# Two transformer blocks on one core: the residual stream with its features on partitions, side work placed by a clock of TensorE time

## The chip, the cores and the metric

One core of a Trainium2 chip runs the whole program in one launch. The metric is the device time of that launch in microseconds, the median of several runs. All arithmetic is fp32 to the outside.

## The reference

One batch of 512 tokens with 1024 features goes through two blocks. The parts that matter here, shortened:

```python
mem_n = rmsnorm(mem, mem_norm)
# layer A (mLSTM)
h = rmsnorm(x, a_norm)
qk, v, o, z, i_pre, f_pre, mq, mz = split_cols(h @ a_w_in, ...)
ht = mlstm_chunkwise(q, k, v, i_pre + ig_b, f_pre + fg_b)      # 4 heads of 256
x = x + concat(sigmoid(o) * rmsnorm(ht) * silu(z), memory_attention(mq, mz, mk, mv)) @ a_w_out
# layer B (MLA)
c_kv, k_pe = split_cols(rmsnorm(x, kv_norm) @ w_kv_a, ...)     # k, v of 8 heads from the latent
q_lat, z, mq, mz = split_cols(rmsnorm(x, b_norm) @ b_w_in, ...)
x = x + concat(chunk_causal_attention(q, k, v) * silu(z), memory_attention(mq, mz, mk, mv)) @ b_w_out
# second block
u, q, k, v, gates = split(rms_norm(x, g_mix) @ w_in, ...)
x = x + (concat(causal_multiscale_pool(u), rms_norm(diff_attention(q, k, v))) * sigmoid(gates)) @ w_out
x = x + memory_cross_attention(rms_norm(x, g_cross), rms_norm(mem_2, g_mem))
x = x + square(relu(rms_norm(x, g_mlp) @ w_up)) @ w_down       # 4096 wide
return rms_norm(x, g_final)
```

A norm multiplies each token by 1/sqrt(mean of its squares) and each feature by a gain. memory_attention and cross attention see 256 memory tokens.

## The kernel before

**Products.** Every large product is an entry of product_table: a weight, its columns, its source and a form. Weights come in chunks of two k tiles (128 rows of the weight each); SP fetches a chunk into one of two raw buffers, ScalarE writes its upper half (split, hi), VectorE the rest (lo = raw - hi), into one of three w_split slots. The source (hA, hB, ...) lies in actA or actB as hi and lo too, with features on partitions. For every k tile and every one of up to four output blocks, TensorE does three matmuls: hi hi, hi lo, lo hi. In "feature" form the weight block is stationary and the result has features on partitions; in "token" form the source block is stationary and the result has tokens on partitions. The four blocks of a product fill the PSUM banks 0 to 3 and are evicted (ev) when the last k tile is done.

**The residual stream** x_res is 128 x 4 x 1024: tokens on partitions, four token tiles. The residual products (outA, outB, outC, outD, dn0 to dn3, two halves each) are in token form and are added to it; ScalarE sums the squares of each block as it lands (rsq). Before the next layer each feature tile must be turned: turn is four transposes (two for the memory's 256 tokens) on TensorE (line L1019, in turn_over), then ScalarE writes hi from PSUM, times the feature gain (L1330), and VectorE lo (L1720). The factor per token is applied after the product: nsum makes the mean, POOL takes the power -0.5 (L2267), and where tokens lie along the free axis, ndiag and nrow (a diagonal times a matrix of ones) spread it over all partitions into row[norm].

**Side work** is everything else on TensorE: attention scores, turned probabilities, values, mLSTM rounds, gates. It uses the banks 4 to 7. The names: msc, mtp, mval are scores, turn and values of memory attention; asc, atp, aval of MLA; dsc, dtp, dval of differential attention; csc, ctp, cval of cross attention; hsc, hval, hty of the mLSTM; prep0 to prep6 norm, rotate and turn q and k of a pair of MLA heads; hnsq, hnt, hnsc are head norms; ysplit writes hi and lo of a gated output, the source of outA, outB and outC.

**The order** is written once by order_of_work with a Plan, and all five engines walk through the same list. There are two lanes of side work, each a queue of groups with steps they come after, and a list soon. After each k tile of a product, step puts the first group of soon and at most one group of each lane:

```python
    def step(self):
        if self.soon:
            for step in self.soon.popleft():
                self.put(step)
        for lane in (1, 0):
            self.advance(lane)
```

need(steps) calls step until the steps are there; product calls it for the source tiles of each k tile (hA, hB and the like two tiles ahead). All twelve matmuls of a k tile stand together in TensorE's queue. In rounds, the scores of unit n and the turn of unit n - 1 are one group, with two buffers for probabilities.

**The start:** mem, then x (512 KB per token tile), memT and hA turned, products mk0, mv0, mqA, mzA. The forget gates of the mLSTM need a cumulative sum and a cumulative maximum over 512 tokens; each is nine doubling steps of two VectorE operations over 4 x 512 (cumsum, cummax), one doubling per step of lane 1, and gateT turns the result. **The end:** dn31 is evicted, its squares summed, each token tile scaled and stored.

## Time and profile before

| | |
|---|---|
| median of 3 runs | 1754.74 us (1748.2 to 1758.79) |
| the profiled execution | 1747.94 us |
| its span, first to last instruction | 1746.0 us |
| TensorE busy | 1629.9 us, 7336 matmuls |
| VectorE busy | 889.9 us |
| ScalarE busy | 753.1 us |
| POOL busy | 69.9 us |
| mean granted clock of TensorE | 0.974 |
| HBM read | 138.17 MB, 80 GB/s over the span |

Busy time of TensorE counts overlapping matmuls once; a single matmul's recorded duration reaches into the next one, so costs are read from the distance of starts. "idle before" is time in which the engine had nothing to do, put down to what it waited for. The span ends some 2 us before the execution's own time.

### The profile page before, as it was taken

To read this page: it belongs to the slowest core of one execution; us is meant where nothing else is said; L and a number is where in the kernel's file an instruction comes from. 1 tells how busy PE (TensorE), PEld (TensorE's weight loads), DVE (VectorE), ACT (ScalarE), POOL (GpSimd) and SP (SyncE) were. 2 spreads that over 40 slices of the span, in tenths; PEclk is the share of its full clock that TensorE was granted. 3 is DMA by queue.
4 is the path that set the end of the run, shared out by engine and by line. 5 is a ranking of instruction groups with operands and counts; after the bars stand their busy time and mean duration, and the time that the engine had idled before them with its cause. 6 is when DMAs were issued, how large, how long until landed. Compare 5 with 4: busy or idle time off the path is not lost.

```text
span 1746.0 us, 19776 instructions
## 1 busy us (share of the span) xinstructions
PE 1629.9 (93%) x7336; PEld 1269.4 (73%) x7336; DVE 889.9 (51%) x1879; ACT 753.1 (43%) x1714; POOL 69.9 (4%) x64
## 2 busy tenths in 40 slices
PE   6996999999999978899899999889999999999997
PEld 5574777777787866666678877467786878888886
DVE  4367446738445464555544647445444453434343
ACT  6353333324345556666433343335323443434342
POOL 0011001101000000000000000000000000000000
PEclk9998999999999999999999999689999999999999
DMA  6221222222333211111123222013232323333332
GB/s 202 72 82 37 73 61 73 84 62 86 132 103 115 67 38 50 45 46 47 61 74 108 85 73 85 1 50 108 86 108 79 103 85 98 97 100 95 98 98 78
DMA packets 85119, 141.54 MB, mean 81 GB/s; under 512 B 7200, under 2 KB 32160, under 8 KB 85024
## 3 DMA queue, kind: packets, MB, share of 16 engines
q1 hardware_dynamic: 83728, 137.45, 25.5%
q10 hardware_dynamic: 1296, 2.83, 0.5%
q8 instruction: 58, 0.95, 0.2%
q14 instruction: 37, 0.30, 0.1%
HBM read 138.17 MB, written 2.10 MB: 80 GB/s over the span
## 4 chain that ended last, share of the span: by engine, by line
PE 61%; DVE 13%; issue 13%; ACT 10%; DMA 1%; POOL 1%; ACTq 0%; DVEq 0%; SPq 0%; POOLq 0%
PE banks L1059 10%; PE banks L1061 10%; PE banks L1060 10%; PE banks L1054 7%; PE banks L1056 7%; PE banks L1055 7%; DVE sb_arena L1711 3%; ACT sb_junk L1318 3%; PE banks L1019 3%; DVE sb_arena L1720 2%; DVE sb_w_split L1711 2%; ACT sb_w_split L1355 2%; ACT sb_arena L1484 1%; PE banks L1243 1%; DVE sb_arena L1714 1%
## 5 line engine op out<-in xcount | busy, mean ns | idle before, releaser
L1711 DVE TENSOR_TENSOR sb_w_split<-sb_raw,sb_w_split 128x512 fp32r<-128x512 f32 (+4 forms) x520 | 322.6, 662 | 367.2 <-ACT sb_w_split L1355 366.3
L1355 ACT ACTIVATE sb_w_split<-sb_raw 128x512 fp32r<-128x512 f32 (+4 forms) x520 | 286.1, 600 | 352.7 <-PE banks L1061 193.3
L1059 PE MATMUL banks<-sb_w_split,sb_actB 128*128 128x512 f32 (+2 forms) x752 | 302.3, 402 | 7.2 <-DVE sb_w_split L1711 3.0
L1061 PE MATMUL banks<-sb_w_split,sb_actB 128*128 128x512 f32 (+2 forms) x752 | 291.5, 388 | 0.0
L1060 PE MATMUL banks<-sb_w_split,sb_actB 128*128 128x512 f32 (+2 forms) x752 | 291.2, 387 | 0.0
L1054 PE MATMUL banks<-sb_actA,sb_w_split 128*128 128x512 f32 x672 | 271.9, 405 | 1.6 <-DVE sb_arena L1720 1.5
L1056 PE MATMUL banks<-sb_actA,sb_w_split 128*128 128x512 f32 x672 | 262.9, 391 | 0.0
L1055 PE MATMUL banks<-sb_actA,sb_w_split 128*128 128x512 f32 x672 | 262.5, 391 | 0.0
L1059 PE MATMUL banks<-sb_w_split,sb_actA 128*128 128x512 f32 (+1 forms) x416 | 167.8, 403 | 2.2 <-DVE sb_arena L1720 2.2
L1059 PEld LDWEIGHTS banks<-sb_w_split,sb_actB 128*128 128x128 f32 x752 | 144.0, 192 | 32.9 <-DVE sb_w_split L1711 5.6
L1061 PEld LDWEIGHTS banks<-sb_w_split,sb_actB 128*128 128x128 f32 x752 | 143.1, 190 | 28.2
L1060 PEld LDWEIGHTS banks<-sb_w_split,sb_actB 128*128 128x128 f32 x752 | 143.9, 191 | 25.1 <-issue 0.5
L1061 PE MATMUL banks<-sb_w_split,sb_actA 128*128 128x512 f32 (+1 forms) x416 | 161.2, 387 | 0.0
L1060 PE MATMUL banks<-sb_w_split,sb_actA 128*128 128x512 f32 (+1 forms) x416 | 160.8, 386 | 0.0
L1019 PE MATMUL banks<-sb_cons,sb_arena 128*128 128x128 f32 x508 | 94.6, 294 | 65.8 <-DVE sb_arena L1714 35.9
L1054 PEld LDWEIGHTS banks<-sb_actA,sb_w_split 128*128 128x128 f32 x672 | 126.7, 188 | 27.7 <-issue 3.6
L1056 PEld LDWEIGHTS banks<-sb_actA,sb_w_split 128*128 128x128 f32 x672 | 126.5, 188 | 27.5
L1055 PEld LDWEIGHTS banks<-sb_actA,sb_w_split 128*128 128x128 f32 x672 | 126.8, 189 | 25.4 <-issue 1.0
L1019 PEld LDWEIGHTS banks<-sb_cons,sb_arena 128*128 128x128 f32 x508 | 63.9, 148 | 97.9 <-DVE sb_arena L1714 42.4
L2267 POOL TENSOR_TENSOR sb_small<-sb_small,sb_cons 128x4 f32<-128x4 f32 (+4 forms) x33 | 44.0, 1336 | 1556.0 <-DVE sb_small L1717 1556.0
L1484 ACT ACTIVATE sb_arena<-banks,sb_small 128x256 f32<-128x256 f32 (+2 forms) x80 | 45.3, 567 | 126.6 <-DVE sb_small L1714 126.4
L1059 PEld LDWEIGHTS banks<-sb_w_split,sb_actA 128*128 128x128 f32 x416 | 78.6, 189 | 22.2 <-issue 5.3
(163 smaller groups left out, 1864.1 us busy)
## 6 DMA issues: line engine op xcount, KB each, us to landing
sb_raw<-in_a_w_in SPq DMA_DIRECT2D x64, 256.0 KB, 3.0
sb_raw<-in_w_up SPq DMA_DIRECT2D x32, 512.0 KB, 3.6
sb_raw<-in_w_down SPq DMA_DIRECT2D x32, 512.0 KB, 3.7
sb_raw<-in_w_in SPq DMA_DIRECT2D x24, 512.0 KB, 3.6
sb_raw<-in_mem_w_kv SPq DMA_DIRECT2D x16, 512.0 KB, 3.8
sb_raw<-in_a_w_in SPq DMA_DIRECT2D x16, 512.0 KB, 3.7
sb_raw<-in_w_ckv SPq DMA_DIRECT2D x16, 512.0 KB, 3.7
sb_raw<-in_a_w_out SPq DMA_DIRECT2D x12, 512.0 KB, 3.7
```

The source lines that it names most:

```text
L1019: t = pe.op.transpose(v.ps[0:rows, place.bank, n * P:(n + 1) * P], block, v.ident)
L1054: pe.op.matmul(out, hi[:, cs], x.hi(k), start=i == 0, stop=False)
L1055: pe.op.matmul(out, hi[:, cs], x.lo(k), start=False, stop=False)
L1056: t = pe.op.matmul(out, lo[:, cs], x.hi(k), start=False, stop=last_i)
L1059: pe.op.matmul(out, x.hi(k)[:, cs], hi, start=i == 0, stop=False)
L1060: pe.op.matmul(out, x.hi(k)[:, cs], lo, start=False, stop=False)
L1061: t = pe.op.matmul(out, x.lo(k)[:, cs], hi, start=False, stop=last_i)
L1318: t = act.op.activation(v.junk[:, 0:src.shape[-1]], src, ACT.Square, accum_out=out)
L1355: act.op.activation(hi[:, cs], raw[:, cs], ACT.Copy).then_inc(act.mark(m("w_hi"), 2 * n + part + 1), 1)
L1484: act.op.activation(prob, src, ACT.Exp, bias=v.stat(("mx", step), 1), scale=scale, accum_out=v.stat(("sm", step), 1)).then_inc(act.mark(em ...
L1711: dve.op.tensor_tensor(out, a, b, op).then_inc(dve.mark(*mark) if mark else dve.tick(), 1)
L2267: pool.op.tensor_tensor(v.stat(root, n), v.stat(mean, n), v.con("minus_half", 0, n), ALU.pow).then_inc(m.at("rstd", step)[0], 1)
```

## The change

The residual stream and the three memory inputs are kept with features on partitions (x_res is 128 x 8 x 512; x, mem and mem_2 come transposed from the host, and the output is handed back so). The residual products take the feature form. turn becomes one ScalarE operation (hi, from SBUF) and one VectorE operation (lo). The squares of a feature tile are taken by ScalarE (sqa), added up over the tiles by POOL (sqp) and summed over partitions by matmuls of one column (nsq). The final norm takes the same way, with nrow, and eight stores of a feature tile.

In the order, Plan has a clock: row_ns and side_ns estimate TensorE's time of each row block and each side step, and a group of a lane is put only when its lag has passed since the last one of that lane. The row blocks of a k tile are steps of their own (rows), and a group of one lane can be put between them. need takes only what is missing (force). Units of layer B's attention have two groups between scores and turn, with three buffers; mzB is two products, the products of layer B stand in another order, the sum and the maximum of the gates are one scan each (gateA), mqA is the first product, and x is loaded one feature tile at a time beside the first chunks. ckD1 is before cqD0, and cvD0 and cvD1 are behind cqD1.

The diff, cut to its core (the lists of addresses, buffers and waits that follow from it are left out):

```diff
-    add("mzB", B, D_MODEL, [(B_MZ, 512)], "feature", "hB", "silu")
+    for n in range(2):
+        add(f"mzB{n}", B, D_MODEL, [(B_MZ + n * 256, 256)], "feature", "hB", "silu")
...
-            add(f"{name}{half}", w, nk * P, [(half * 512, 512)], "token", src, "res", order=order, k0=k0)
+            add(f"{name}{half}", w, nk * P, [(half * 512, 512)], "feature", src, "res", order=order, k0=k0)
...
+def row_ns(name):
+
+    pr = PRODUCTS[name]
+    return 3 * n_out(name) * ((pr.tokens if pr.form == "feature" else wide(name)) / 2.4 + 13)
...
+def side_ns(step):
+
+    kind, i = step[0], step[-1]
+    wide_f32, turn = 1.68, 109
+    if kind in ("msc", "mtp"):
+        return 430 if kind == "msc" else 2 * turn
+    if kind in ("csc", "ctp"):
+        return 860 if kind == "csc" else 2 * turn
+    if kind in ("mval", "cval"):
+        return 2 * 860 if kind == "mval" else 4 * 860
+    if kind == "asc":
+        return (i + 1) * P * (wide_f32 + 2.1) + 66
+    if kind == "dsc":
+        return 2 * ((i + 1) * P * 3.0 + 66)
+    if kind in ("atp", "dtp"):
+        return (i + 1) * turn
+    if kind == "dval":
+        return (i + 1) * 224
+    if kind == "hsc":
+        return (TT - i) * P * wide_f32 * 3 + 66
+    if kind == "hval":
+        return (i + 1) * (430 + 224)
+    return {"aval": 10 * P * wide_f32, "gate0": 3440, "gate1": 3440, "gate2": 3440, "gate3": 3440, "pp": 860,
+            "nsq": 900, "nrow": 860, "gateT": 660}.get(kind, TT * turn if kind in EMPTIES else 0)
...
+def squares(norm, n):
+
+    return [("sqa", norm, n)] + ([("sqp", norm, n)] if n and not (norm == "f" and n >= 4) else [])
...
+        self.clock, self.last = 0.0, [0, 0]
...
+        self.clock += side_ns(step)
...
-    def side(self, lane, after, *steps):
-        self.lanes[lane].append((tuple(after), steps))
+    def side(self, lane, after, *steps, lag=2600):
+
+
+        self.lanes[lane].append((tuple(after), steps, lag + (LATER.get(steps[0], 0) if steps else 0)))
+
+    def take(self, lane):
+        self.last[lane] = self.clock
+        for step in self.lanes[lane].popleft()[1]:
+            self.put_side(lane, step)
 
     def advance(self, lane):
-        if self.lanes[lane] and all(a in self.done for a in self.lanes[lane][0][0]):
-            for step in self.lanes[lane].popleft()[1]:
-                self.put_side(lane, step)
+        if self.lanes[lane]:
+            after, steps, lag = self.lanes[lane][0]
+            if all(a in self.done for a in after) and self.clock - self.last[lane] >= lag:
+                self.take(lane)
...
+    def force(self, step):
+
+        if any(step in group for group in self.soon):
+            for s in self.soon.popleft():
+                self.put(s)
+            return
+        lane = next((n for n in (0, 1) if any(step in group[1] for group in self.lanes[n])), None)
+        assert lane is not None, ("nothing to wait for", step)
+        missing = [a for a in self.lanes[lane][0][0] if a not in self.done]
+        if missing:
+            self.force(missing[0])
+        else:
+            self.take(lane)
...
     def need(self, *steps):
-        tries = 0
-        while not all(s in self.done for s in steps):
-            tries += 1
-            assert tries < 1000, ("nothing to wait for", [s for s in steps if s not in self.done])
-            self.step()
-
-    def product(self, name, before_ev=(), soon=None):
+        for step in steps:
+            while step not in self.done:
+                self.force(step)
...
-                banks = [(j, EV_EMPTIES[pr.ev]) for j in range(n_out(name))] if i == 0 else ()
+                banks = [(into[j], EV_EMPTIES[pr.ev]) for j in range(n_out(name))] if i == 0 else ()
                 self.put(("mm", name, i), banks)
+                for j in range(n_out(name)):
+                    self.put(("rows", name, i, j))
+                    self.clock += row_ns(name) / n_out(name)
+                    if j < n_out(name) - 1:
+                        self.advance((i * n_out(name) + j) % 2)
...
+    def after_residual(self, name):
+
+        norm, turn, first = NORM_AFTER[name[:-1]], TURN_AFTER.get(name[:-1]), 4 * int(name[-1])
+        for j in range(first, first + 4):
+            steps = [("turn", turn, j)] if turn else []
+            if first:
+                for step in steps:
+                    self.put(step)
+                self.soon.append(squares(norm, j))
+            else:
+                self.soon.append(steps + squares(norm, j))
...
-    def scales(lane, norm, row=True, after=()):
-        p.side(lane, after, ("nsum", norm))
+    def turns(name, tiles):
+
+        for k in tiles:
+            p.soon.append([("turn", name, k)])
+
+    def scales(lane, norm, row=True, after=(), lag=4000):
+        p.side(lane, after, lag=0)
+        p.side(lane, (), ("nsq", norm), ("nsum", norm), lag=lag)
         if row:
-            p.side(lane, ())
-            p.side(lane, (), ("ndiag", norm))
-            p.side(lane, (), ("nrow", norm))
+            p.side(lane, (), ("ndiag", norm), ("nrow", norm), lag=4500)
...
+        complete, first = None, True
+        for n in range(len(units) + depth):
...
-                group.append((turn_over, *before))
-                if before[-1] == TT - 1:
-                    complete = before[:-1]
-            before = u
-            p.side(lane, after if first else values_after if group[0][0] == values else (), *group)
+            if n < len(units):
+                group.append((scores, *units[n]))
+            if n >= depth:
+                u = units[n - depth]
+                group.append((turn_over, *u))
+                if u[-1] == TT - 1:
+                    complete = u[:-1]
+            p.side(lane, after if first else values_after if group[0][0] == values else (), *group, lag=lag)
             first = False
...
+    for n in range(2):
+        p.put(("load_x", n))
+        p.put(("fetch", n))
+    p.n_fetch = 2
+    p.put(("load_x", 2))
+    p.put(("turn", "hA", 0))
+    p.put(("split", 0))
+    p.put(("fetch", 2))
+    p.put(("load_x", 3))
+    p.put(("turn", "hA", 1))
...
+        p.soon.append(([("turn", "hA", k)] if k >= 2 else []) + squares("a", k))
+    for n in range(4):
+        p.soon.append([("turn", "memT", 2 * n), ("turn", "memT", 2 * n + 1)] + squares("mem", n))
+    p.soon.append([("masks",)])
+    scales(0, "a", after=[("sqp", "a", 7)], lag=0)
...
+    p.product("mqA", [("nsum", "a")])
+    p.ahead = SPLIT_SLOTS
+    scales(0, "mem", row=False, after=[("sqp", "mem", 3)])
+    p.product("mk0", [("nsum", "mem")], into=(5, 7))
...
-    p.side(1, (), ("gateL",))
-    for n in range(9):
-        p.side(1, (), ("cumsum", n))
     p.side(1, (), ("gateA",))
-    for n in range(9):
-        p.side(1, (), ("cummax", n))
-    p.side(1, (), ("gateM",))
-    p.side(1, (), ("gateT",))
-    p.product("mqA", [("nsum", "a")])
-    head_norm(0, "mqA", TT, True)
+    p.side(1, (), ("gateT",), lag=4000)
...
-            p.side(1, after if si == 0 else (), *group)
+            p.side(1, after if si == 0 else (), *group, lag=5000)
...
-    turns(1, "memTb", range(KD))
     p.product("outA0")
-    turns(0, "hB", range(4))
+    p.put(("load_mem_again",))
     p.product("outA1")
 
 
     p.put(("enter", "outA1"))
-    turns(0, "hK", range(KD))
-    scales(0, "b")
+    turns("hK", range(KD))
+    scales(0, "b", after=[("sqp", "b", 7)])
+    for k in range(KD):
+        p.soon.append([("turn", "memTb", k)])
+    p.product("qlB", [("nsum", "b")])
+    for step in (("qll0",), ("qll1",)):
+        p.side(1, (), step, lag=1500)
+    p.product("ckvB")
+    for step in (("kvl0",), ("kvl1",)):
+        p.side(1, (), step, lag=1500)
     p.product("mk1")
-    head_norm(1, "mk1", MT, False)
+    head_norm(0, "mk1", MT, False)
     p.product("mv1")
     for n in range(3):
...
+    def mla(h0):
+
+        units = [(h, j) for h in (h0, h0 + 1) for j in range(TT)]
+        complete = None
+        for n in range(len(units) + 3):
+            group, after = [], []
             if complete is not None:
                 group += [("aval", complete), ("ysplit", "yB", complete)]
+                after.append(("silu", f"zB{complete // 2}", complete % 2))
...
+            if n < len(units):
+                group.append(("asc", *units[n]))
+                after.append(("prep6", h0 // 2))
+            if 2 <= n < len(units) + 2:
+                group.append(("atp", *units[n - 2]))
+                if units[n - 2][1] == TT - 1:
+                    complete = units[n - 2][0]
+            p.side(0, after, *group, lag=2800)
+
+    def mem_b(h0):
+        rounds(0, [("B", h, i) for h in (h0, h0 + 1) for i in range(TT)], "msc", "mtp", "mval",
+               [("hnscale", "mqB"), ("hnt", "mk1", 3)], [("silu", f"mzB{h0 // 2}", 1)], depth=2, lag=2400)
...
-            p.side(1, (), (f"prep{s}", q))
-        p.product(f"zB{q}", (), lambda j: [(("silu", f"zB{q}", j),)])
+        for n in range(7):
+            p.side(1, (), (f"prep{n}", q), lag=2600)
+
+    def gated(name):
+        p.product(name, (), lambda j: [(("silu", name, j),)])
+
+    gated("zB0")
+    p.need(("kpe",))
+    latents(0)
+    p.product("mqB")
+    mla(0)
+    head_norm(1, "mqB", TT, True)
+    mem_b(0)
+    mem_b(2)
+    latents(1)
+    p.need(("nrow", "b"))
+    gated("mzB0")
+    gated("mzB1")
+    mla(2)
+    latents(2)
+    p.need(("mval", "B", 3))
+    gated("zB1")
+    mla(4)
+    latents(3)
+    p.need(("ysplit", "yB", 1))
+    gated("zB2")
+    p.need(("ysplit", "yB", 3))
+    gated("zB3")
+    mla(6)
     for h in range(MEM_HEADS):
...
+        elif kind == "nsq":
+            norm = a[0]
+            tiles, place_full = v.tiles_of[norm], open_bank(step)
+            place, full = place_full
+            blocks = [(v.sq_sum[norm], 0)] if tiles == TT else [(v.sq_sum[norm], 0), (v.sq_sum[norm], N_MEM)]
+            last = SQUARES.get(norm, KD) - 1
+            if norm == "f":
+                blocks += [(v.square_of(norm, n)[1], 0) for n in range(4, KD)]
+                pe.wait_ge(*m.at("sq", ("sqa", norm, last)))
+                last = 3
+            pe.wait_ge(*m.at("sq_sum", ("sqp", norm, last)))
+            for i in range(tiles):
+                for n, (block, at) in enumerate(blocks):
+                    t = pe.op.matmul(v.ps[:, place.bank, i:i + 1], block[:, at + i * P:at + (i + 1) * P], v.con("ones"),
+                                     start=n == 0, stop=n == len(blocks) - 1)
...
+            act.op.activation(dst.hi(k), src, ACT.Copy, scale=gain).then_inc(act.mark(*m.at("t_hi", step)), 1)
+        elif kind == "sqa":
+            norm, n = a
+            src, out = v.square_of(norm, n)
...
+            back = 5 if norm == "f" else 2
+            if n > back:
+                act.wait_ge(*m.at("sq_sum", ("sqp", norm, n - back)))
+            act.op.activation(out, src, ACT.Square).then_inc(act.mark(*m.at("sq", step)), 1)
...
+            dve.wait_ge(*m.at("t_hi", step))
+            fused(dst.lo(k), src, gain, ALU.mult, dst.hi(k).bitcast(F32), ALU.subtract, *m.at("t_lo", step))
...
-        elif kind == "gateA":
-            g = v.gate_rows
+            dve.op.memset(g[7], 1.0).then_inc(dve.tick(), 1)
+            dve.settle()
+            dve.op.tensor_tensor_scan(g[6], g[7], g[5], 0.0, ALU.mult, ALU.add).then_inc(dve.tick(), 1)
             dve.settle()
             tensor(g[1], g[0], g[6], ALU.subtract)
             dve.settle()
-            copy(g[2], g[1])
-        elif kind == "cummax":
-            doubling(a[0], (2, 3), ALU.max)
-        elif kind == "gateM":
-            g = v.gate_rows
-            dve.settle()
-            both(v.neg_m, g[3], 0.0, ALU.max, -1.0, ALU.mult)
+            dve.op.tensor_tensor_scan(g[3], g[1], g[1], 0.0, ALU.max, ALU.max).then_inc(dve.tick(), 1)
+            dve.settle()
+            scalar(v.neg_m, g[3], -1.0, ALU.mult)
...
+        elif kind == "sqp":
+            norm, n = a
+            signal, value = m.at("sq_sum", step)
+            pool.wait_ge(*m.at("sq", ("sqa", norm, n)))
+            if n >= 2:
+                pool.wait_ge(signal, value - 1)
+            total = v.sq_sum[norm]
+            pool.op.tensor_tensor(total, total, v.square_of(norm, n)[1], ALU.add).then_inc(signal, 1)
```

## Rows read from the trace of the kernel before

**Rows 1.** Stretches in us: length; busy PE, PEld, DVE, ACT, POOL; granted clock; DMA share; GB/s.

```profile
0.00:50.00 50.00, 34.14 (x155) 26.91 (x155) 25.79 (x54) 33.77 (x84) 4.32 (x13) 0.97 0.60 194
50.00:200.00 150.00, 131.50 (x530) 94.18 (x529) 83.34 (x192) 61.16 (x144) 9.60 (x5) 0.93 0.21 60
200.00:500.00 300.00, 295.95 (x1336) 231.68 (x1335) 163.91 (x317) 104.96 (x197) 23.08 (x16) 1.00 0.27 84
500.00:850.00 350.00, 312.98 (x1501) 238.47 (x1499) 193.04 (x482) 212.84 (x566) 22.27 (x14) 0.99 0.21 62
850.00:1050.00 200.00, 197.75 (x891) 154.83 (x892) 98.77 (x210) 73.94 (x159) 1.16 (x2) 0.99 0.26 80
1050.00:1150.00 100.00, 89.22 (x328) 59.28 (x327) 58.11 (x147) 33.78 (x95) 3.02 (x3) 0.80 0.13 42
1150.00:1450.00 300.00, 282.30 (x1345) 227.46 (x1344) 142.61 (x285) 119.72 (x255) 4.18 (x7) 0.99 0.29 92
1450.00:1735.00 285.00, 285.00 (x1259) 235.99 (x1258) 118.93 (x182) 107.76 (x205) 0.00 (x0) 1.00 0.29 91
...
sum 1746.00, PE 1629.93 PEld 1269.38 DVE 889.94 ACT 753.07 POOL 69.89; mean PE 181.10 PEld 141.04 DVE 98.88 ACT 83.67 POOL 7.77
```

**Rows 2.** TensorE's timeline at 25 us: start, us, line, form.

```profile
25.00 0.39 PE L1060 MATMUL banks<-sb_w_split,sb_actB 128*128 128x512 f32 x1
25.23 0.39 PE L1061 MATMUL banks<-sb_w_split,sb_actB 128*128 128x512 f32 x1
25.46 0.60 PE L1019 MATMUL banks<-sb_cons,sb_x_res 128*128 128x128 f32 x4
25.81 0.48 PE L1059 MATMUL banks<-sb_w_split,sb_actB 128*128 128x512 f32 x1
26.13 0.40 PE L1060 MATMUL banks<-sb_w_split,sb_actB 128*128 128x512 f32 x1
```

**Rows 3.** TensorE's waits between 500 and 850 us: total, times, longest.

```profile
PE banks L1019 <- DVE sb_arena L1714: 13.0, 7, 3.3
PE banks L1019 <- DVE sb_arena L1711: 10.9, 8, 1.8
```

**Rows 4.** TensorE's timeline at the gates, after 159 us.

```profile
159.79 0.98 PE L1123 MATMUL banks<-sb_cons,sb_arena 4*128 4x4 f32 x8 [3.39 <-DVE sb_arena L1711]
...
162.58 0.63 PE L1060 MATMUL banks<-sb_w_split,sb_actA 128*128 128x512 f32 x1
163.01 0.63 PE L1061 MATMUL banks<-sb_w_split,sb_actA 128*128 128x512 f32 x1
```

**Rows 5.** Groups by line on TensorE: count, busy us, mean ns, idle before.

```profile
L1019 PE MATMUL banks<-sb_cons,sb_x_res 128*128 128x128 f32 x192 | 29.2, 275 | 0.9 <-DVE sb_actA L1720 0.9
...
L1173 PE MATMUL banks<-sb_cons,sb_arena 128*128 128x1 f32 x80 | 9.8, 234 | 0.0
```

**Rows 6.** Timelines of VectorE and POOL while both work on SBUF.

```profile
265.14 2.33 DVE L1720 SCALAR_TENSOR_TENSOR sb_arena<-sb_arena,sb_cols 128x512 f32<-128x512 f32 x3
...
267.96 4.15 DVE L1720 SCALAR_TENSOR_TENSOR sb_arena<-sb_arena,sb_cols 128x512 f32<-128x512 f32 x3
...
268.11 3.45 POOL L2285 TENSOR_TENSOR sb_arena<-sb_arena 128x512 f32<-128x512 f32 x2 [16.56 <-ACT sb_arena L1500]
```

**Rows 7.** Groups by line and shape, on POOL and on VectorE.

```profile
L2267 POOL TENSOR_TENSOR sb_small<-sb_small,sb_cons 128x4 f32<-128x4 f32 x15 | 15.1, 1007 | 846.6 <-DVE sb_small L1717 846.6
...
L1711 DVE TENSOR_TENSOR sb_arena<-sb_arena 4x512 f32<-4x512 f32 x3 | 2.0, 680 | 2.9 <-ACT sb_arena L1460 2.9
```

**Rows 8.** TensorE's timeline in the first stretch: first product, and wait behind mk0.

```profile
14.52 0.80 PE L1059 MATMUL banks<-sb_w_split,sb_actB 128*128 128x512 f32 x1 [3.02 <-DVE sb_w_split L1711]
...
31.65 0.68 PE L1059 MATMUL banks<-sb_w_split,sb_actB 128*128 128x512 f32 x1 [1.93 <-ACT sb_arena L1394]
```

**Rows 9.** Timelines of TensorE and VectorE at the end.

```profile
1735.71 0.39 PE L1061 MATMUL banks<-sb_w_split,sb_actB 128*128 128x512 f32 x1
...
1738.28 2.73 DVE L1720 SCALAR_TENSOR_TENSOR sb_arena<-sb_x_res,sb_small,sb_arena 128x512 f32<-128x512 f32 x4
```

554 lines of the change are left out of this document (254 added, 300 removed).

## The prediction

> **What bounds the kernel now.** I read the profile from the whole to the place. First the table of stages [rows 1]. TensorE is busy 1629.9 of 1746.0 us, and VectorE and ScalarE each about half of that, so only TensorE's queue sets the end: either something leaves that queue, or one of its waits goes. The differences (length less busy) are its idle time: 15.9 us in the first 50 us, 18.5 in 50 to 200, 4.1 in 200 to 500, 37.0 in 500 to 850, 2.2 in 850 to 1050, 10.8 in 1050 to 1150, 17.7 in 1150 to 1450, none in the long MLP stretch; of the 116.1 us in total, 9.9 are left for what follows the last product. The granted clock falls below 1.00 where there are waits: 0.93 in 50 to 200 and 0.80 in 1050 to 1150.
>
> Second, what a product costs when nothing disturbs it: two neighbouring 128x512 matmuls start 0.23 us apart [rows 2]. The same rows price a turn: with four transposes between them, the matmuls of 25.23 and 26.13 are 0.90 us apart where two pitches would be 0.46. The four cost 0.44 us, 0.11 us each, though each is recorded with some 0.27 us (they overlap).
>
> Third, what the waits in the stages are. Between 500 and 850 us nearly all are transposes (line L1019) that wait for VectorE's scaling of a softmax block (L1714, L1711) [rows 3]: 13.0 + 10.9 us. That is a round whose scores, exponentials and turn follow each other in TensorE's queue faster than VectorE and ScalarE get through them. Between 50 and 200 us it is the same kind plus the forget gates: TensorE stands 3.39 us before the turn of the gate rows, and what follows then runs at the low one of the clock's two levels, 1.2 instead of 2.4 GHz: pitch 0.43 us [rows 4].
>
> **The change part by part, against the profiled span of 1746.0 us.**
>
> *Transposes of the normalised streams go.* With features on partitions, turn is one ScalarE and one VectorE operation from SBUF; TensorE has no part in it. Removed are 8 x 2 for each of memT, memTb and m2T and 8 x 4 for each of hA, hB, hK, hC, hD, hE: 48 + 192 [rows 5] = 240. Eight of them lie in the idle start. 232 x 0.11 = -25.5 us, in the open, since TensorE is otherwise busy there. The residual products keep their count and size; only the operands change sides, the same stationary block still serves two matmuls of three: 0. On the other engines a turn keeps its two operations, and the sums of squares of dn0 to dn2, which nobody reads, go: less work on ScalarE, behind TensorE, 0.
>
> The Trainium skill (TensorE: Matmul & The Clock Gate, Part 4: PE-mode transpose) gives about 275 ns for a 128x128 transpose in one kernel. The records agree with that length, the pitch does not: by 0.275 the 232 would be worth an estimated 64 us instead of 25.5.
>
> *Sums of squares over partitions come.* Seven norms ahead of the last get nsq: 28 matmuls of one column. The one-column matmuls of this trace are recorded with 0.234 us [rows 5]; the pitch of a short one is nearer 0.11. 3.1 to 6.6 us; I take +3, since they have a transpose's weight load. ScalarE squares into a ring, POOL adds: 7 adds for each of a to e, 3 for f, mem and m2, 44 in all. A 128x512 POOL operation took 1.7 us beside VectorE, and three VectorE operations beside two of these took 4.15 us where three took 2.33 alone [rows 6]: 0.9 us of VectorE per add, 40 us spread over the kernel. VectorE is idle half of the time [rows 1], and the weight split runs two to three chunks (5.4 us each) ahead of TensorE: I take 0 for it; with the cover gone, at a border where evictions, turns and splits queue behind each other, up to 4 x 0.9 at five borders, +18.
>
> The Trainium skill (SBUF — State Buffer, SBUF: two separate sides) says that a VectorE operation with two SBUF inputs and a GpSimd operation that reads SBUF exclude each other for the whole instruction. The new VectorE half of turn, the split and ysplit are all of that form. By that rule each add could hold VectorE for its full 1.7 us, an estimate of 75 us of VectorE time instead of 40; still hidden while VectorE has half its time free.
>
> *The chain behind each residual.* Four evictions, squares, adds, nsq, nsum, the POOL root (1.0 us, [rows 7]), ndiag, nrow must be through before the next product is evicted. Cover: kC and up00 have 96 matmuls, 21.8 us; qlB 96 of 384 columns, about 16.6; ckD0 of 256 tokens about 11, and with it m2's squares, put last. Two places force their nsq and nrow into the end of the product: I count +3 at ckD0 and 0 elsewhere; it is in the term of 1150 to 1450. In return the first tiles no longer wait for turns there.
>
> *Start.* TensorE's first product begins at 14.52 [rows 8], after 1 MB of mem, eight turns of one bank lane and the split. Afterwards it waits for one 256 KB tile of x, one chunk and its split. The core moved 194 GB/s on average in this stretch [rows 1]; x, cons and the first chunk, some 1.2 MB, land about 6 us in, the split adds 2.5: about 8.5. -6 us, and -1 for the 1.9 us wait behind mk0. Bounds 0 (loads stay the limit: mqA needs 0.5 MB per 2.7 us of products, 190 GB/s, as much as was moved) and -11.
>
> *50 to 200 us.* Cumsum and cummax, 36 dependent VectorE operations over 4x512, one pair per tile of TensorE's order, become two scans. The trace has no scan; its price is bounded by one operation (0.68 us, [rows 7]) and by the 18 x 0.68 that it replaces. One is nearest in shape; the gates are then ready long before ozA0. The memory rounds take 4.4 us of TensorE time per group instead of 2.7 plus their own. Of 18.5 idle I take 15, and 5 more for the low clock: -20 (bounds -8, -25).
>
> *500 to 850 us.* The mem rounds of layer B get two groups between scores and turn, three buffers for probabilities, and lie behind the first MLA heads; MLA likewise; prep is spread. A chain waits for ScalarE and VectorE for 1 to 3.3 us a time, and one more group of 2.4 to 2.8 us covers that. Of 37.0 I take 29, and 2 for the clock: -31 (bounds -10, -36). If the cover fails, it is in outB0, where the last heads are forced: then they wait there.
>
> *1050 to 1150 us.* The differential attention still waits for gateG of gC0 and is then forced before outC0: the burst stays. -3 (0 to -10). *1150 to 1450:* turns at two borders, cross attention over both lanes. Of 17.7 I take 12, less 3 at ckD0: -9 (+3 to -15). *200 to 500, 850 to 1050, MLP:* 6.3 us idle, 0.
>
> *Tail.* The last matmul starts at 1735.71 [rows 9] and ends 0.23 later: 10.1 us to the end. Afterwards: eviction 0.7, square 0.6, 20 one-column matmuls 2.2, nsum 0.3, root 1.0, ndiag 0.9, nrow 1.1, its copy 0.6, eight stores at 0.69 (four took 2.73, [rows 9]) 5.5, last landing 3, hand-overs 1: 17. +7 (5 to 10), all open.
>
> **Sum:** -25.5 + 3 - 7 - 20 - 31 - 3 - 9 + 7 = -85.5, so a span of 1660.5. The profiled execution took 1747.94, 1.9 more than its span: 1662.4, a ratio of 0.951. The median before is 1754.74; by the ratio 1669, by the difference to the lower one 1662. I say 1665.
>
> **Rivals.**
> *A, the order helps half:* the chains stay bound by VectorE's and ScalarE's own queues, in front of which evictions and splits stand, and only the low ends (8, 10) of the two large terms come. 1665 + 12 + 21 = 1698. For: VectorE is at 50 to 60% in both windows, and POOL's adds come on top. Against: waits are at most 3.3 us, less than a group.
> *B, the places are worth nothing:* what is forced by need stands as before. Only turns, start, sums and tail: -25.5 + 3 - 7 + 7 = -22.5, 1729.
> *C, more:* nearly all inner idle time and low clock go, 15 to 40 us beyond the forecast: 1637.
> *D, transposes cost TensorE their recorded length* [rows 5] where the trace's pitch is not looked at: 232 x (0.27 - 0.11) = 37 more, 1628. Against it is the pitch of [rows 2]. (It is the case that the 275 ns of the Trainium skill, TensorE: Matmul & The Clock Gate, would give.)
> *E, slower:* the norm chain is not covered at the five residual borders. It decides when a chain overruns its product by more than 85.5/5 = 17 us at each; with 20 us, 1665 + 100 = 1765. That needs a chain of 36 us and more; its parts above sum to about 10, and with both lags of 4.0 and 4.5 us to 20.
>
> **Chances.** Forecast (1645 to 1688) 0.58; A 0.18; B 0.06; C 0.10; D 0.02; E 0.04; about no change 0.02. The bounds of the terms alone give 1630 to 1718; range 1628 to 1705, which leaves out B, E, the no-change case and the far ends. 0.5% (9 us) is what a measurement of this kernel tells from no change: faster 0.94, same 0.02, slower 0.04.
>
> **What would show it.** No L1019 rows from x_res or mem (right); the next products' pitch still 0.23; idle time of 500 to 850 under 10 us; no wait before gateT; start of the first product before 10 us; tail of 15 to 20 us. Wrong would be: long waits of TensorE for nsq or nrow, splits late behind POOL's adds (a wait on w_split's lower half), or new waits in outB0 and outC0.

## Result, and the profile after

The changed kernel took **1784.7 us** (median of 4 runs, 1784.0 to 1787.7); the kernel before, timed beside it, took 1754.2. The ratio is **1.0178, 95% interval 1.0149 to 1.0206**: 30 us slower. Forecast was 1665 us, faster. The profiled execution took 1784.0 us with a span of 1782.2.

The same stretches of the changed kernel as in [rows 1], with the same columns:

```profile
50.00:200.00 150.00, 127.96 (x509) 91.86 (x508) 74.12 (x152) 67.59 (x158) 10.42 (x6) 0.93 0.25 69
200.00:500.00 300.00, 298.68 (x1331) 232.94 (x1329) 168.35 (x328) 104.10 (x199) 26.00 (x19) 1.00 0.28 83
500.00:850.00 350.00, 308.08 (x1395) 232.06 (x1393) 194.86 (x487) 209.24 (x567) 28.88 (x18) 0.94 0.21 59
...
1150.00:1450.00 300.00, 277.41 (x1260) 220.99 (x1260) 151.16 (x290) 113.82 (x241) 30.62 (x25) 0.95 0.28 85
...
sum 1782.00, PE 1648.46 PEld 1274.07 DVE 911.12 ACT 732.44 POOL 132.27; mean PE 206.06 PEld 159.26 DVE 113.89 ACT 91.55 POOL 16.53
```

Read it against [rows 1]. The idle time of 500 to 850 us is 41.9 us, not under 10 (before: 37.0); in 50 to 200 it is 22.0 (18.5); in 1150 to 1450 it is 22.6 (17.7). The granted clock fell in two of the three, 0.99 to 0.94 and 0.99 to 0.95; in 50 to 200 it stayed at 0.93. And TensorE is busy 18 us *longer* with 142 matmuls fewer.

Fixed stretches mix up stages as soon as one kernel runs ahead, so for all that follows I cut both traces by products: TensorE's timeline gives the start of each product's first matmul, the program's order says which product it is, and a stage is the distance between two such starts. Each distance from one matmul's start to the next is booked on product, side work or, where the timeline shows a wait, idle time. In us (the last column is the best version found, e15 below):

| stage | before | changed | difference | e15 |
| --- | --- | --- | --- | --- |
| start to qkA1 | 223.3 | 216.3 | -7.0 | 210.0 |
| qkA1 to layer B | 288.0 | 283.7 | -4.3 | 285.2 |
| layer B to outB0 | 324.9 | 344.4 | **+19.5** | 329.4 |
| outB0, outB1 | 92.8 | 90.6 | -2.2 | 90.0 |
| layer C | 274.1 | 277.8 | +3.7 | 273.0 |
| layer D | 180.1 | 191.4 | **+11.3** | 182.3 |
| MLP to dn31 | 331.0 | 335.5 | +4.5 | 328.7 |
| dn31 to the end | 31.8 | 42.5 | **+10.7** | 39.8 |
| sum | 1746.0 | 1782.2 | +36.2 | 1738.4 |

By kind, from the same cut, in us:

| | before | changed | e15 |
| --- | --- | --- | --- |
| up to the first product | 14.5 | 8.0 | 8.0 |
| product matmuls | 1307.9 | 1337.0 | 1316.9 |
| side work | 320.0 | 304.0 | 302.7 |
| idle | 93.3 | 112.8 | 92.6 |
| from the last product matmul's start | 10.3 | 20.4 | 18.3 |

Idle time is here what the profile puts before TensorE's matmuls between the first and the last product. In the side work, all transposes on TensorE together fell from 73.7 us (700 of them) to 49.7 (460): 24.0 for the 240 that left (eight of them before the first product), near the 25.5 that I forecast. Of the 29 us by which product matmuls rose, 17 are at the low clock (distance between starts over 0.36 us; the time above 0.227 each sums to 19.7 before, 37.2 after). Layer B's 19.5 us are 7.7 of idle time, 1.3 of side work and 10.5 in product matmuls, nearly all of it at the low clock (0.4 before, 10.7 after).

The three places where the loss shows best are these. TensorE's timeline in quB2, where the rest of layer B's memory rounds is forced (7 of the 16 units stand there, and quB2 takes 26.9 us in place of 13.5):

```profile
714.49 0.41 PE L1214 MATMUL banks<-sb_w_split,sb_actB 128*128 128x384 f32 x1 [2.74 <-ACT sb_arena L1588]
...
726.56 0.66 PE L1172 MATMUL banks<-sb_cons,sb_arena 128*128 128x128 f32 x2 [1.97 <-ACT sb_arena L1646]
728.75 3.75 PE L1304 MATMUL banks<-sb_actB_plain 128*128 128x512 f32 x4 [1.53 <-ACT sb_actB_plain L1656]
...
737.37 0.69 PE L1172 MATMUL banks<-sb_cons,sb_arena 128*128 128x128 f32 x2 [1.47 <-DVE sb_arena L1869]
```

TensorE's in ckD0, the norm of the second memory, and under it POOL's timeline of that moment:

```profile
1233.62 1.83 PE L1241 MATMUL banks<-sb_cons,sb_arena 128*128 128x1 f32 x8 [9.30 <-POOL sb_arena L2404]
1237.27 1.19 PE L1250 MATMUL banks<-sb_arena 128*128 128x256 f32 x2 [1.81 <-DVE sb_arena L1869]
1239.48 0.55 PE L1209 MATMUL banks<-sb_actB,sb_w_split 128*128 128x256 f32 x1 [1.02 <-DVE sb_arena L1866]
```

```profile
1224.76 8.71 POOL L2404 TENSOR_TENSOR sb_arena<-sb_arena 128x512 f32<-128x512 f32 x6 [3.63 <-ACT sb_arena L1550]
```

Six adds in a row, 1.45 us each: three for the residual's own norm (d), then the three of the second memory, for the last of which TensorE waits. They start late, too. ScalarE's timeline just before shows the squares of the residual behind a weight split whose weights had not landed:

```profile
1223.01 1.16 ACT L1509 ACTIVATE sb_w_split<-sb_raw 128x512 fp32r<-128x512 f32 x2 [4.31 <-DMA sb_raw<-in_w_ckv]
1224.07 1.13 ACT L1550 ACTIVATE sb_arena<-sb_x_res 128x512 f32<-128x512 f32 x2
```

And the tail; with [rows 9]:

```profile
1761.84 0.40 PE L1211 MATMUL banks<-sb_actB,sb_w_split 128*128 128x512 f32 x1
1763.73 5.25 PE L1241 MATMUL banks<-sb_cons,sb_arena 128*128 128x1 f32 x40 [1.49 <-issue]
1771.48 2.04 PE L1250 MATMUL banks<-sb_arena 128*128 128x512 f32 x2 [2.51 <-POOL sb_arena L2406]
```

I had counted 20 one-column matmuls, 2.2 us. They took 5.25 us, 0.26 us each; each shows as two records.

### The profile page after: what moved, and what is told of

It reads as the page before. It is cut to its first block, busy times and chain, and to the rows that moved or that the text cites. A ratio compares the mean times of both kernels' runs of the same rounds, so it can differ in the third digit from the quotient of the medians.

```text
span 1782.2 us, 19350 instructions
## 1 busy us (share of the span) xinstructions
PE 1648.5 (92%) x7194; PEld 1274.1 (71%) x7194; DVE 911.1 (51%) x1853; ACT 732.4 (41%) x1619; POOL 132.3 (7%) x106
## 4 chain that ended last, share of the span: by engine, by line
PE 71%; DVE 13%; ACT 8%; issue 4%; DMA 2%; POOL 1%; ACTq 0%; DVEq 0%; POOLq 0%; SPq 0%
PE banks L1209 15%; PE banks L1211 15%; PE banks L1210 15%; PE banks L1214 5%; PE banks L1216 5%; PE banks L1215 5%; DVE sb_arena L1866 3%; DVE sb_w_split L1866 3%; PE banks L1172 2%; ACT sb_junk L1477 2%; DVE sb_arena L1875 2%; PE banks L1401 2%; ACT sb_arena L1646 1%; ACT sb_w_split L1509 1%; DMA sb_raw<-in_mem_w_kv 1%
## 5 line engine op out<-in xcount | busy, mean ns | idle before, releaser
L1866 DVE TENSOR_TENSOR sb_w_split<-sb_raw,sb_w_split 128x512 fp32r<-128x512 f32 (+3 forms) x530 | 339.3, 682 | 392.6 <-ACT sb_w_split L1509 391.2
L1509 ACT ACTIVATE sb_w_split<-sb_raw 128x512 fp32r<-128x512 f32 (+3 forms) x530 | 288.0, 593 | 469.0 <-PE banks L1211 359.7
L1209 PE MATMUL banks<-sb_actA,sb_w_split 128*128 128x512 f32 x672 | 276.8, 412 | 6.4 <-DVE sb_arena L1866 3.1
L1211 PE MATMUL banks<-sb_actA,sb_w_split 128*128 128x512 f32 x672 | 264.7, 394 | 0.0
L1210 PE MATMUL banks<-sb_actA,sb_w_split 128*128 128x512 f32 x672 | 263.9, 393 | 0.0
L1209 PE MATMUL banks<-sb_actB,sb_w_split 128*128 128x512 f32 (+1 forms) x640 | 255.4, 399 | 5.6 <-DVE sb_actB L1866 2.2
L1211 PE MATMUL banks<-sb_actB,sb_w_split 128*128 128x512 f32 (+1 forms) x640 | 249.6, 390 | 0.0
L1210 PE MATMUL banks<-sb_actB,sb_w_split 128*128 128x512 f32 (+1 forms) x640 | 249.3, 389 | 0.0
L1214 PE MATMUL banks<-sb_w_split,sb_actA 128*128 128x512 f32 (+1 forms) x384 | 157.0, 409 | 12.6 <-DVE sb_w_split L1866 9.1
L1209 PEld LDWEIGHTS banks<-sb_actA,sb_w_split 128*128 128x128 f32 x672 | 127.9, 190 | 36.2 <-issue 10.0
L1215 PE MATMUL banks<-sb_w_split,sb_actA 128*128 128x512 f32 (+1 forms) x384 | 151.5, 394 | 0.0
L1216 PE MATMUL banks<-sb_w_split,sb_actA 128*128 128x512 f32 (+1 forms) x384 | 151.2, 394 | 0.0
L1209 PEld LDWEIGHTS banks<-sb_actB,sb_w_split 128*128 128x128 f32 x640 | 123.7, 193 | 34.2 <-issue 6.5
L1211 PEld LDWEIGHTS banks<-sb_actA,sb_w_split 128*128 128x128 f32 x672 | 127.3, 189 | 27.7
L1210 PEld LDWEIGHTS banks<-sb_actA,sb_w_split 128*128 128x128 f32 x672 | 127.9, 190 | 25.5 <-issue 1.5
L1210 PEld LDWEIGHTS banks<-sb_actB,sb_w_split 128*128 128x128 f32 x640 | 123.4, 193 | 26.8 <-issue 1.4
L1211 PEld LDWEIGHTS banks<-sb_actB,sb_w_split 128*128 128x128 f32 x640 | 123.0, 192 | 27.0
L1172 PE MATMUL banks<-sb_cons,sb_arena 128*128 128x128 f32 x460 | 83.7, 292 | 47.2 <-DVE sb_arena L1869 16.9
L2404 POOL TENSOR_TENSOR sb_arena<-sb_arena 128x512 f32<-128x512 f32 x44 | 64.9, 1477 | 710.2 <-ACT sb_arena L1550 707.2
L1172 PEld LDWEIGHTS banks<-sb_cons,sb_arena 128*128 128x128 f32 x460 | 58.7, 149 | 70.6 <-issue 22.6
L2395 POOL TENSOR_TENSOR sb_small<-sb_small,sb_cons 128x4 f32<-128x4 f32 (+3 forms) x30 | 41.8, 1394 | 789.8 <-DVE sb_small L1872 740.9
```

The costliest lines, as they stand in the source:

```text
L1172: t = pe.op.transpose(v.ps[0:rows, place.bank, n * P:(n + 1) * P], block, v.ident)
L1209: pe.op.matmul(out, hi[:, cs], x.hi(k), start=i == 0, stop=False)
L1210: pe.op.matmul(out, hi[:, cs], x.lo(k), start=False, stop=False)
L1211: t = pe.op.matmul(out, lo[:, cs], x.hi(k), start=False, stop=last_i)
L1214: pe.op.matmul(out, x.hi(k)[:, cs], hi, start=i == 0, stop=False)
L1215: pe.op.matmul(out, x.hi(k)[:, cs], lo, start=False, stop=False)
```

## The experiments

Ratios are to the kernel before, timed beside each run; the changed kernel's is 1.0178. e1 to e8 ran on one chip, e9 to e11 on a second, e12 to e14 on a third and e15 on a fourth, so across these groups the ratios compare better than the medians.

| run | median us | ratio | 95% interval |
| --- | --- | --- | --- |
| e1 pace of before | 1779.2 | 1.0148 | 1.0124 to 1.0173 |
| e2 no places | 1768.7 | 1.0088 | 1.0062 to 1.0114 |
| e3 second memory's sums first | 1777.4 | 1.0143 | 1.0122 to 1.0165 |
| e4 layer B's old order | 1801.3 | 1.0276 | 1.0255 to 1.0298 |
| e5 actA and actB exchanged | 1759.6 | 1.0044 | 1.0027 to 1.0061 |
| e6 rounds of B spread | 1763.1 | 1.0064 | 1.0042 to 1.0086 |
| e7 gates earlier | 1760.7 | 1.0044 | 1.0021 to 1.0068 |
| e8 POOL's sums twice | 1774.6 | 1.0127 | 1.0103 to 1.0150 |
| e9 actB where it was, tail | 1746.1 | 0.9961 | 0.9944 to 0.9979 |
| e10 gates and B mended | 1753.4 | 1.0008 | 0.9993 to 1.0022 |
| e11 e9 and e10 | 1743.0 | 0.9945 | 0.9927 to 0.9962 |
| e12 wide cover for B | 1739.4 | 0.9923 | 0.9903 to 0.9942 |
| e13 before, 136 transposes less | 1742.9 | 0.9942 | 0.9920 to 0.9965 |
| e14 before, 240 transposes more | 1770.8 | 1.0096 | 1.0073 to 1.0120 |
| e15 best order | 1737.2 | 0.9916 | 0.9898 to 0.9934 |

**e1 and e2: the pace, and the places.**

```diff
-                    if j < n_out(name) - 1:                       # e1 and e2
-                        self.advance((i * n_out(name) + j) % 2)
-            if all(...) and self.clock - self.last[lane] >= lag:  # e1 only
+            if all(...):
```

> The changed kernel with the pace of the kernel before: a group of each lane is released after every k tile, whatever the clock says, and none between the row blocks of a k tile. Product order, layout and norm steps stay as changed. Theory 1 (the lags and the places between row blocks are what went wrong: they hold side work back until a product needs it all at once): the 19.5 us that layer B lost and most of the extra low-clock time (17 us) come back, 1745 to 1760 us, against 1784.7 for the changed kernel. Theory 2 (the pace is worth what it was meant to be, and layer B lost its time to the new order of its products): bursts of short work make it slower still, 1795 to 1815 us. Theory 3 (neither: layout and norm chains cost it): within 8 us of 1784.7.

> Lags kept, but no group is placed between the row blocks of a k tile: groups come only at the end of a k tile, when their lag has passed. Theory 1 in the form that the places break up the products (each place leaves two short pieces of product and a gap in which the clock falls): 1765 to 1775 us, with fewer stretches of product matmuls at 0.43 us. Theory 2 (places help): 1790 to 1800 us. Theory 3: within 5 us of 1784.7.

e1 took 1779.2, e2 1768.7 us. None of the theories has it right for both: e1 lies where theory 3 had it, e2 where theory 1 had it, but the time at the low clock, which theory 1 wanted down, hardly fell (37.2 to 34.8 us). The places between row blocks cost: without them the ratio is 0.0090 lower, 16 us. By stages, 10 of them came before qkA1 (qkA0 took 47.6 us in place of 54.0, vA0 30.8 in place of 37.1), 4 each in layers B and C, and qkA1 to layer B gave 3 back. In layer C the places are what made TensorE wait: kC, qC and vC took 24.2, 23.8 and 24.3 us in e2, as before, and in the changed kernel 27.7, 25.9 and 27.6, with these waits:

```profile
955.46 2.05 PE L1250 MATMUL banks<-sb_arena 128*128 128x512 f32 x2 [2.31 <-DVE sb_arena L1869]
976.48 0.66 PE L1172 MATMUL banks<-sb_cons,sb_arena 128*128 128x128 f32 x4 [2.07 <-DVE sb_arena L1866]
1002.46 0.73 PE L1172 MATMUL banks<-sb_cons,sb_arena 128*128 128x128 f32 x4 [2.10 <-DVE sb_arena L1866]
```

As I read it, a place in the middle of a k tile brings a group forward, in front of the last row blocks that would have covered its chain; no run shows this apart. The lags, on the other hand, help: e1 differs from e2 by them alone and is 10.5 us slower. Layer B did not come back in either (344.2 and 340.7 us).

**e3: the order of two sums on POOL.**

```diff
-    for n in range(4):
-        p.soon.append(squares("m2", n))
+    p.soon.extendleft([squares("m2", n) for n in (3, 2, 1, 0)])
```

> The squares of the second memory are put ahead of the squares of the residual at the start of layer D. The 9.30 us wait of the first one-column matmuls of that norm behind POOL's sums in ckD0 goes away if the order of POOL's queue was its cause: ckD0 from 26.6 to 16 to 18 us, the kernel 1774 to 1778 us. If the wait was for the arrival of the memory's data instead, ckD0 stays at 25 to 27 us and the time at 1783 to 1786. Should the wait move on to the residual's own norm (first used by cqD0, two products later), cqD0 gets an idle time over 3 us.

The wait of 9.30 us is gone, ckD0 took 18.9 us, layer D 181.4 in place of 191.4, and the ratio fell by 0.0035, 6 us. The order in which the squares and sums are queued was the cause. It is not all POOL's: ScalarE's wait of 4.31 us for the weights, which had held up the residual's squares and with them the sums of m2, is now 0.92 and behind m2's squares. In the new order a turn of m2T came late instead (TensorE waited 2.01 us for it), and waits of 2.58 us for the row (nrow) and 1.02 behind it stayed.

**e4: layer B's old order** (mqB and mzB ahead of the latents, one round behind, all in lane 0).

> Layer B's order of products and of side work is taken back as far as the buffers allow (all memory rounds in lane 0, turned over one unit after their scores, products mqB and mzB ahead of the latents, attention turned over one unit late), with the new lags and places. Theory 2 (the new order of layer B costs it 19.5 us): layer B from the start of qlB to outB0 falls from 344.4 to about 325 us, the kernel to 1763 to 1768 us. Theory 1 (the pace costs it): layer B stays at 340 to 350 us, the kernel within 6 us of 1784.7.

Layer B took 354 us, 10 more: the rounds then have to end in quB0, which took 49.1 us (15.0 idle). Theory 2 as I had put it fell. The new order was not the loss as a whole. In the changed layout the old one cannot be had: the allocation puts the turned probabilities into actB, where ckvB's operand hK still is, so that the rounds can begin only when ckvB is through; before, ckvB stood beside 6 of the 16 units. qlB, which stood beside 8, is free of that (e12 below puts it there).

**e5 to e8** stand on e2 and e3 together, a base that was not run alone.

> From here on the base is the changed kernel with e2 and e3 together: no places between row blocks, the second memory's squares first. If the two add up, that base runs about 1768.7 - 7 = 1762 us. On it, this run exchanges the addresses of the two buffers of split activations in SBUF, and nothing else. In the changed kernel a down product takes 22.4 us (pitch 0.2333 us) and an up product 21.8 us (0.2267), both in feature form; before, both took 21.8. Theory A (the address of the moving operand sets the pitch): after the exchange up products take 22.4 and down products 21.8 us. Theory B (it is what else runs during down products, the residual's adds and squares): nothing changes, down 22.4, up 21.8. Theory C (the distance between the two operands or which of them lies lower): both change or both become alike.

TensorE's timeline of the changed kernel in an up product, then in a down product:

```profile
1599.90 0.39 PE L1210 MATMUL banks<-sb_actA,sb_w_split 128*128 128x512 f32 x1
...
1600.58 0.39 PE L1210 MATMUL banks<-sb_actA,sb_w_split 128*128 128x512 f32 x1
...
1639.65 0.39 PE L1210 MATMUL banks<-sb_actB,sb_w_split 128*128 128x512 f32 x1
...
1640.35 0.40 PE L1210 MATMUL banks<-sb_actB,sb_w_split 128*128 128x512 f32 x1
```

and of e5:

```profile
1589.82 0.40 PE L1206 MATMUL banks<-sb_actA,sb_w_split 128*128 128x512 f32 x1
...
1590.52 0.39 PE L1206 MATMUL banks<-sb_actA,sb_w_split 128*128 128x512 f32 x1
...
1634.93 0.39 PE L1208 MATMUL banks<-sb_actB,sb_w_split 128*128 128x512 f32 x1
...
1635.61 0.39 PE L1208 MATMUL banks<-sb_actB,sb_w_split 128*128 128x512 f32 x1
```

Three pitches are 0.68 us from actA and 0.70 from actB in the changed kernel, and the other way round in e5. Over whole products: up 21.8 and down 22.4 became up 22.4 and down 21.8. Theory A holds, to the last product: the pitch goes with the place in SBUF. Products in token form, which hold actA still and move the weights, rose too (ozA1 24.45 us in e2 and in the changed kernel, 25.06 in e5).

> On the same base, layer B's products in the order qlB, ckvB, mqB, mk1, mzB0, mv1, mzB1, then the latents of each pair of heads and its zB, so that the memory rounds of layer B start at the end of mzB0 and are over at the end of quB0, none of them forced; the norms of mqB and mk1 are spaced 1.2 us, the memory rounds 1.2 us. The theory that layer B lost its 19.5 us to the burst that is forced in quB2 (26.9 us for a product of 6.5, 9.7 of them idle) and to rounds that follow each other too closely there: the stretch from qlB to outB0 falls from 340.8 us (e2) to 320 to 328 us and the kernel to 1742 to 1750 us. The rival, that the side work of layer B waits for ScalarE and VectorE wherever it stands: the stretch stays at 335 to 345 us, the idle time moves to mv1, mzB1 and quB0.

The theory fell in this form: layer B took 346.8 us. Nothing was forced, but mv1 took 32.6 us with 11.1 idle and kvB0 waited 6.83 us. Part of that was my own order: the rotary tables stood among the rounds, and the latents right before their reader.

> On the same base, the loads of the gate weights go ahead of mk0 and the gates' matmuls, scans and transposes go behind mk0, ahead of that product's norm, so that they run during mv0 and mzA in place of qkA0. The theory that layer A gained nothing in the stretch 50 to 200 us because mk0 and mv0 now run with no side work beside them and everything waits in qkA0 and ozA0: the waits at gateT (3.3 us) and before msc and hval there (6 us) go, outA0 starts at 402 to 408 us instead of 413, the kernel 1752 to 1757 us. The rival, that the memory rounds wait for the softmax on ScalarE and VectorE whatever the gates do: outA0 at 411 to 415 us and the time at 1760 to 1764.

The time was that of e5, 1760.7 against 1759.6 us. The stretch from the first product to ozA1 took 244.2 us, against 240.6 in e5, and outA0 began at 418.6 us, later than either case had it. The waits at the gates went, and as much came in mzA, where a bank waited 5.58 us to be read out by VectorE, which was busy with the gates' scans. VectorE's work is only moved.

> On the same base, GpSimd makes each of its 44 additions of squares a second time (384 of 512 columns, into a buffer that nobody reads), some 50 us of additional work on GpSimd beside VectorE. My prediction costed GpSimd's sums at nothing. If that holds, the kernel stays within 4 us of its base (1762 us). If GpSimd's additions delay VectorE's work that TensorE waits for, or the norm chains wait for the last sum, each of the six chains gets 1 to 2 us longer and the kernel 1768 to 1780 us; half of such a rise would then be in the changed kernel too.

The upper case: 15 us slower than e5, 14 than e7. e5 also has the two buffers exchanged, so the stages are better read against e2, and ckD0 against e7: the first product mqA +3.4, qlB +5.8, kC +3.6, ckD0 +3.6, up00 +0.3, outD0 0. These are the borders. At qlB (2.87 us) and kC (1.74) TensorE waits for the last sum:

```profile
510.48 1.84 PE L1238 MATMUL banks<-sb_cons,sb_arena 128*128 128x1 f32 x8 [2.87 <-POOL sb_arena L2407]
```

At mqA and ckD0 it waits for VectorE's own work, a weight split (2.93 us, 1.17 in e2) and a turn's lower half (3.54, 2.07 in e7), both stretched beside POOL's adds: the two split halves before the first of these waits took 2.98 us, 2.06 in e2.

**e9: actB back behind actA, and the last norm's sums in four banks.** The first half of the edit moves the allocation of actB from the end to its place before; the second is

```diff
+    for n, (block, at) in enumerate(blocks):       # one wait per block, not one for all
+        if n: pe.wait_ge(*m.at("sq", ("sqa", norm, n + 3)))
+        for i in range(tiles): pe.op.matmul(v.ps[:, 4 + i, 0:1], ...)
```

> On the base of e5 to e8 two edits that act in different stretches. First, the second buffer of split activations (actB) goes back to where the kernel before had it in SBUF, right behind actA, and the weights' buffers go up by its size; in the changed kernel it lay at the end. e5 showed that the slow pitch (0.2333 us against 0.2267) goes with the place. Theory A (a buffer at the far end is read more slowly, one near the start is not): up, down and out products all at 0.2267, a down product 21.8 us, outA1 and outB1 32.6, together 9 to 11 us less. Theory C (one of the two buffers is always the slow one): down stays at 22.4 or up becomes so, 0 us. Second, the last norm: the sums over the 128 partitions of the five blocks are kept in four banks of their own, so that all but the last block's are made before the last square is there. The run of 40 one-column matmuls in 5.25 us behind the last square becomes 8 in about 1.1 us: the tail from the start of dn31 goes from 42.5 to about 38.5 us. Both together: 1759.6 - 10 - 4 = 1745 to 1748 us; 1755 to 1757 if theory C holds.

1746.1 us, 13.5 less than e5 (14.5 by the ratios). Up, down and out products all run at 0.2267 us (21.8 us; outA1 and outB1 32.6). The tail came to 40.2 us, not 38.5: its 20 matmuls (40 records) now begin right behind the last product and still end 5.13 us later.

```profile
1725.92 5.13 PE L1242 MATMUL banks<-sb_cons,sb_arena 128*128 128x1 f32 x40
1733.60 2.05 PE L1258 MATMUL banks<-sb_arena 128*128 128x512 f32 x2 [2.56 <-DVE sb_arena L1877]
```

They are not bound by the last square, as I had thought: it ended at 1727.47, 3.6 us before the last of them. The loads of their 40 blocks fill the same time, 5.26 us. The tail gave 2.3 us, which leaves 11 for the place of the buffer, against e5, where actA stood at the end. e10 and e11 differ by the same two edits, with actB at the end in e10, on one chip: 10.4 us, of which the tail has 3.3. So the place of actB is worth 7 to 11 us.

> On the base of e5 to e8, the orders of e6 and e7 with their own faults mended. In e7 gateT came one k tile behind gateA and waited 5.6 us; it now comes behind the norm of mk0. In e6 the rotary tables (8 loads of ScalarE's table) stood among the memory rounds, which waited 5.2 and 2.7 us for ScalarE, and the turned latents came right before the product that reads them (6.8 us); now the tables go beside mqB and the latents beside mzB1. Theory (orders can take back what layers A and B lost): outA0 at 400 to 405 us against 413 to 418; layer B from qlB to outB0 at 322 to 330 us against 340; the kernel 1735 to 1742 us. Rival (with the buffers of the changed layout, layer B has only narrow products beside its memory rounds, and stands at 340 whatever the order): layer B 337 to 345 us, waits between mv1 and quB0 of 10 us or more, the kernel 1750 to 1756 us.

Between the two: 1753.4 us. Layer B took 334.6 us, the first product to ozA1 242.1 (240.6 in e5, nothing gained). The expectation had misread one row of e7: the wait of 5.6 us was that of mzA's bank, not gateT's, and with gateT later it was there again.

> e9 and e10 together, with e2 and e3 in it: the version that the runs so far point to. If the parts add up it stands at 1720 to 1730 us if e10's theory holds, and at 1736 to 1742 us if its rival does; either beats the kernel before (1751 to 1754 us) and the changed kernel (1784.7 us). If moving the weights' buffers up slows the token products (their moving operand is the weights), they show 0.2333 us in place of 0.2267 and the gain of e9's first half is halved.

1743.0 us; the parts (13.5 and 6.2 us less than e5) add up but for 3 us. The products in token form, which move the weights, kept their pitch (ozA1 24.45 us). Here is what paces a memory round, from ScalarE's and VectorE's timelines in mv1:

```profile
595.96 0.42 DVE L2085 TENSOR_REDUCE sb_small<-banks 128x1 f32<-128x256 f32 x1 [0.22 <-PE banks L1295]
596.42 0.21 DVE L1874 TENSOR_SCALAR sb_small<-sb_small 128x1 f32<-128x1 f32 x1
596.73 0.57 ACT L1651 ACTIVATE sb_arena<-banks,sb_small 128x256 f32<-128x256 f32 x1 [1.30 <-DVE sb_small L1874]
597.42 0.16 DVE L2089 RECIPROCAL sb_small<-sb_small 128x1 f32<-128x1 f32 x1 [0.79 <-ACT sb_arena L1651]
597.62 0.35 DVE L1874 TENSOR_SCALAR sb_arena<-sb_arena,sb_small 128x256 f32<-128x256 f32 x1
...
598.68 0.42 DVE L2085 TENSOR_REDUCE sb_small<-banks 128x1 f32<-128x256 f32 x1
```

Each unit is a chain over both engines, 2.7 us from one reduction to the next, with a weight split between. TensorE's own share of a unit is about 1 us, so by this estimate a unit wants some 1.7 us of product beside it, or TensorE waits.

> The version of e11 with one more product moved in layer B: mqB first, and qlB (three sources wide, 17.5 us) between mv1 and mzB1, beside the memory rounds, which are spaced 2.0 us in place of 1.2. In e11 a unit of the memory rounds takes 2.2 to 2.7 us of ScalarE and VectorE in turn, and the rounds stand beside 35 us of narrow products; in the kernel before they stood beside ckvB, qlB and kvB0, 38 us wide. Theory (what is left of layer B's loss is cover: too little product time beside the rounds): the idle time from mzB0 to quB0 (19.9 us in e11) falls to 8 to 12 us, layer B to 322 to 327 us, the kernel to 1732 to 1738 us. Rival (the units are spaced by ScalarE and VectorE, and what is gained at the rounds comes back where their work is late, at the latents and the softmax behind them): layer B 330 to 336 us, the kernel 1740 to 1746 us.

1739.4 us, layer B 329.1 (333.7 in e11): between the two cases in both. The idle time from mzB0 to quB0 fell only from 15.9 to 14.0 us by the profile, not to 8 to 12, and there is a new wait of 7.51 us at mzB0 for ScalarE, in which the rotary tables stood.

> e12 with two corrections that its trace asks for. The rotary tables, whose table loads kept ScalarE from reading out mk1 (7.51 us of waiting at the start of mzB0), go beside ckvB, spread by 4.2 us; and the gates go back to where the changed kernel has them, since e7, e10, e11 and e12 all took 240 to 245 us up to qkA1's end against 239 to 241 with the gates late. If the two waits go and nothing comes in their place: layer B at 322 to 325 us against 329.3, the first 240 us 1 to 3 us shorter, the kernel 1731 to 1735 us. If ScalarE is the bound there and only the place of the wait changes: ckvB grows from 14.1 us to 18 or more and the kernel stays at 1737 to 1741 us.

1737.2 us, the best of all, 2.6% faster than the changed kernel (0.9916/1.0178 = 0.974) and 0.8% faster than the kernel before. But layer B stayed, at 329.4: the wait at mzB0 went from 7.51 to 4.32 us, and what it gave came back in ckvB (0.7 us), mv1 (1.3) and the products behind zB0. Neither case of the expectation holds: ckvB took 14.8 us, not 18, and with the gates back in their place the first product to ozA1 took 242.4 us, 1.2 more than in e12 and not 1 to 3 less. TensorE's longest waits between 500 and 850 us in the best version, and in the changed kernel under them (total, times, longest):

```profile
PE banks L1166 <- DVE sb_arena L1871: 9.1, 3, 3.9
PE banks L1166 <- ACT sb_arena L1651: 5.6, 2, 3.0
PE banks L1166 <- ACT sb_arena L1747: 4.7, 4, 1.9
```

```profile
PE banks L1172 <- ACT sb_arena L1646: 10.3, 9, 2.4
PE banks L1214 <- ACT sb_arena L1588: 5.0, 3, 2.7
PE banks L1172 <- DVE sb_arena L1866: 4.7, 3, 2.9
```

**e13 and e14: the price of a transpose, in the kernel before.**

```diff
-            turn_over(step, [src[:, i, k * P:(k + 1) * P] for i in range(tiles)])
+            pe.op.transpose(v.ps[:, place.bank, i * P:(i + 1) * P], src[...], v.ident)   # e13: only the last i
```

> The kernel before, in which each step that turns a tile of the residual or of the second and third memory on TensorE makes only the last of its transposes (1 of 4, or 1 of 2; the memory's and x's first ones stay whole). 136 of the 232 transposes are left out, so three quarters of each turned tile hold old data; all other work, waits and the order stay. My prediction took each transpose at 0.11 us of the path. If that holds, the time falls by 136 x 0.11 = 15.0 us, to about 1738 us. If the transposes stood in gaps that ScalarE and VectorE set anyway, or kept the clock up, the time falls by less than 5 us.

> The kernel before, in which each such step makes all its transposes twice (232 more, same output). By the price of 0.11 us each on the path: 25.5 us slower, about 1778 us. If the transposes mostly fill gaps: 5 to 12 us slower. Together with e13 this gives the price of one transpose from both sides; the gain that I forecast from their removal rests on it.

136 fewer: 9.3 us less, 0.068 us each (by the interval 6 to 14 us). e14's edit doubles every turn, the eight before the first product with them, so it adds 240 and not 232 (7576 matmuls in its profile, 7336 before): 18.7 us more, 0.078 each (13 to 21). Both lie between my two cases. In the stream the four cost 0.44 us [rows 2]. Where the rest of that price went shows in e13's profile against that of the kernel before, one execution each, cut as above: 14.9 us of side work left, and 6.5 came back in the product matmuls (3.1 at the low clock) and 1.8 as idle time.

## Why the prediction was wrong, step by step

Of its signs, three came: no turns on TensorE from x_res or mem, the first product before 10 us, and, at the edge of 15 to 20 us, a tail of 20.1 behind the last product's end. Three did not: the idle time of 500 to 850 us, the wait before gateT, and the pitch (0.23 from actB as well, but 3% longer, which two decimals hide). Of its signs of being wrong two came, the long wait for nsq (9.30 us) and, once and small, a split late behind POOL's adds (1.14 us at 17.21); outB0 and outC0 wait no longer than before (2.9 and 9.6 us, 3.6 and 10.4).

- **Transposes go, -25.5.** The mechanism is right and the side work fell by 24.0 us. As a gain it was too large: 232 at 0.068 to 0.078 us are 16 to 18 us (e13, e14). The other 7 to 10 us did not come; in e13's profile most of what was missing stood in the product matmuls.
- **Sums over partitions, +3.** Mis-sized: the seven norms' 28 one-column matmuls took 7.4 us (5.7 in e15), 0.20 us each at the full clock.
- **Start, -6.** Right: the first product starts at 8.00 us (forecast 8.5; before 14.52 [rows 8]).
- **50 to 200 us, -20.** Failed: start to layer B gained 11.3 us in all, start and transposes with it. The step said "the gates are then ready long before ozA0". A scan took 1.21 us (bounds 0.68 to 12.2), and the seven VectorE operations that end with the gates' rows 5.6 together, but TensorE still waited 4.59 us:

```profile
127.12 0.98 PE L1281 MATMUL banks<-sb_cons,sb_arena 4*128 4x4 f32 x8 [4.59 <-DVE sb_arena L1866]
```

  The gates' matmuls had moved behind mk0, mv0 and mzA, and stood in qkA0 right before their reader. Moving them up (e7, e10, e11, e12) gained nothing, as VectorE then owed the time elsewhere.
- **500 to 850 us, -31.** The step that failed most; layer B lost 19.5 us (7.7 idle, 10.5 in its product matmuls, at the low clock), 50 off the forecast. It said that "one more group of 2.4 to 2.8 us covers" a wait. I had looked at how far a unit's scores and turn lie apart, and not at what product time stands beside the sixteen units before the first buffer has to be free. The rounds started late, a `need` forced the rest at once, and the forced part waits for the chain of each unit (2.7 us in e11). Nor were "nearly all" waits of that stretch before behind VectorE's scaling: 23.9 of some 35 us were. Spread under a wide product it gives back 10 us (e15 against e9: 339.0 to 329.4), 15 of the 19.5 together with e2 and e3. What keeps layer B 4.5 us above before stays open; the waits that are left are of the same kind, behind VectorE and ScalarE. What brings the low clock into this layer stays open as well. Of my rivals B had it nearest, "what is forced by need stands as before", but it took the forced part to cost no more than before.
- **The places between banks** I took as a help, with no term of their own. They cost some 16 us (e2), most of it before qkA1. The lags help, by about 10 (e1 against e2).
- **1150 to 1450, -9 with +3 at ckD0.** The +3 is the mis-sized term: the wait was 9.30 us, with 1.81 and 1.02 behind it. I wrote that m2's squares come last and priced the lag, and added up neither POOL's queue, three adds of the residual and three of m2 in 8.71 us, nor ScalarE's, which had stood 4.31 us for the weights. e3 gave 6 us of it back.
- **POOL's adds, 0.** Wrong by size. A second set cost 14 to 15 us (e8), all of it at borders. On VectorE the cost came out lower than my 40 us: the split took 719 ns in place of 691, and the lower half of a turn 1079 in place of 750, together 26 us over 446 and 40 instructions. The average hides what happens. Of the 446 split halves 411 overlapped no 128x512 operation of POOL and took 687 ns; the 35 that did took 1099 on average and up to 1819. Of the 40 turns 19 took 745 and the 21 others 1381; the move of their source from PSUM to SBUF costs nothing. The Trainium skill (SBUF — State Buffer, SBUF: two separate sides) has the pair of ports held for the whole instruction, and these rows agree, as do two split halves alone and two beside the six adds:

```profile
1223.67 1.29 DVE L1866 TENSOR_TENSOR sb_w_split<-sb_raw,sb_w_split 128x512 fp32r<-128x512 f32 x2 [2.26 <-ACT sb_w_split L1509]
1225.76 2.57 DVE L1866 TENSOR_TENSOR sb_w_split<-sb_raw,sb_w_split 128x512 fp32r<-128x512 f32 x2 [0.79 <-ACT sb_w_split L1509]
```

  What costs is where they meet: at a border, where TensorE stands behind the last add or behind a split or a turn that an add has held up. "Idle half of the time" had nothing to say about it.
- **"The residual products keep their count and size: 0."** They do, but actB was moved to the end of SBUF by the new layout, and each product that reads it there took 0.6 to 1.0 us more. With its place before, the kernel is 7 to 11 us faster (e9, and e11 against e10). I had read the allocation in the change and costed nothing for it.
- **Tail, +7.** Measured +10.0, the upper bound; the 10.7 of the table has 0.6 of dn31's own. The 20 one-column matmuls took 5.25 us where I had 2.2. The 2.73 us of [rows 9], which I took for four stores, are VectorE's four last operations.
- **Clock.** I had counted 7 us of low clock as won. It was 17 us more instead: 158 product matmuls behind one another at the low clock in place of 84. There are not more waits, 73 in place of 74, they are longer; what sets the low clock off where it is new was not tried.
- **Rival E** was the only slower one, and it is not what happened: no chain overran its product by 17 us. The slower case was many middling losses at once, which I had no rival for. The bounds were also added up wrongly: my own terms give about 1635 to 1727 us, and 1745 with the +18 of POOL's adds, not 1630 to 1718. The result lies outside either.

Taken together: of 85.5 us forecast, the best version shows 7.6 (by the spans): 6.5 at the start, 17.3 of side work and 0.7 of idle time gained, 9.0 lost in product matmuls and 7.9 in the tail. The removal of work came, the tail was paid. The 60 us of waits and low clock that were to go did not go in any of the eleven orders that were run: idle time between the first and the last product is 93 us before, 113 in the changed kernel and 90 to 125 in the others. That the chains over ScalarE and VectorE set this, and no order of TensorE's queue, is what all of them fit; it is not shown by a run of its own, for none shortened such a chain.

## What to carry to other kernels

Do not count the idle time of the engine that sets the end as a stock that a better order can spend: first find the period of the chain that it waits for, and the product time that stands beside all its units until the next forced point. Price a change of layout by where each buffer comes to lie and by each queue, POOL's too, that a norm's last operand passes through, not by the mean load of the engines. And undo a package piece by piece; here the places between row blocks, the order of two sums and the place of one buffer were worth some 30 us together, and hid that the rest is no loss: without those three, and with the last norm's sums in four banks, the kernel is 0.4% faster than the kernel before (e9, interval 0.2 to 0.6).

## What the runs showed of the hardware that I had not expected

- The pitch of back-to-back 128x512 matmuls depends on where in SBUF the activations lie. With both buffers of activations within the first 96 KB of a partition: 0.2267 us. With one of them at the end of all that is allocated, behind the arena: 0.2333 from that one, as moving operand, and about as much more as the block held still. Exchanging two buffers exchanged the pitches (e5), moving one down removed the difference (e9). Where between the two the change lies was not tried; the weights' buffers, at 104 to 128 KB in the kernel before and in e9, move at 0.2267.
- A one-column fp32 matmul with its own 128x128 block shows as two records. Four in a row took 0.81 us, 0.20 each, and 20 in a row 4.80 (e15), 5.13 (e9) and 5.25 us, 0.24 to 0.26 each.
- A VectorE operation with two SBUF inputs can take far longer when it overlaps one of POOL's over 128x512: of 446 split halves the 35 that did took 1.10 us on average and up to 1.82, the others 0.69.
- A scan over 4x512 on VectorE takes 1.21 us, against 0.68 for an operation of that shape.
